# Operand addresses modulo 256 bytes in a two-block transformer kernel's split fp32 matmuls

## The reference, cut to what matters

```
proj = h @ w_in[l]                        # first block: conv, pool and gate branches
mix = merged @ w_out[l]
up = causal_dwconv(h @ w_up[l], w_dw_f[l], b_dw_f[l])
f = (jax.nn.gelu(gt) * v) @ w_down[l]
...
proj = x @ w_in                           # gated delta rule, then swiglu
q, k, v = jnp.split(x @ w_qkv, 3, axis=-1)  # attention, then swiglu
g, u = jnp.split(x @ w13, 2, axis=-1)
return (jax.nn.silu(g) * u) @ w2
```

## The kernel before, in words

| tensor | start before | mod 256 | start in the change | mod 256 |
|---|---|---|---|---|
| raw | 2048 | 0 | 2048 | 0 |
| hi | 47104 | 0 | 47104 | 0 |
| lo | 67584 | 0 | 68224 | 128 |
| ones | 88256 | 192 | 89536 | 192 |
| hh | 89888 | 32 | 91264 | 128 |
| hl | 98080 | 32 | 99456 | 128 |
| fh | 106304 | 64 | 107648 | 128 |
| fl | 110400 | 64 | 111744 | 128 |
| idle | 114496 | 64 | part of ones | 192 |
| crow, xa, h, B, st, ev, Z, sm, cst | 115520 and on | 64 | 116064 and on | 96 |

## Time and profile before

### The profile page before, as it was taken

How to read it: one execution, slowest core, us unless ns; L and a number is a source line. 1 busy time by engine, 2 the same in 40 slices (tenths; PEclk the granted TensorE clock), 3 DMA queues, 4 the chain that set the end, 5 groups by cost and what they waited for, 6 DMA issues and landing times.

```text
span 1039.5 us, 18332 instructions
## 1 busy us (share of the span) xinstructions
PE 1023.4 (98%) x7499; PEld 958.9 (92%) x7499; DVE 754.0 (73%) x1293; ACT 572.9 (55%) x960; POOL 27.5 (3%) x34
## 2 busy tenths in 40 slices
PE   8999999999999999999999999999999999999997
PEld 7999998999999998999987999999899878999996
DVE  6988998899777788877867555555889576555555
ACT  5573447665555586724646445444746565444443
POOL 0000000000100042000000000000000000000000
PEclk9999999999999999999999999999999999999999
DMA  9999873588765533622245555665364426655511
GB/s 370 418 419 370 316 243 124 196 270 274 233 190 193 165 108 115 224 63 80 84 142 186 167 186 191 188 194 186 121 229 158 132 95 250 209 187 183 186 58 41
DMA packets 59603, 201.22 MB, mean 194 GB/s; under 512 B 10496, under 2 KB 10880, under 8 KB 59264
## 3 DMA queue, kind: packets, MB, share of 16 engines
q1 hardware_dynamic: 58368, 199.98, 56.2%
q10 hardware_dynamic: 1152, 0.07, 0.1%
HBM read 198.71 MB, written 1.31 MB: 192 GB/s over the span
## 4 chain that ended last, share of the span: by engine, by line
PE 86%; DVE 10%; ACT 2%; issue 1%; DMA 1%; SPq 0%; DVEq 0%; ACTq 0%
PE ps L632 73%; PE ps L1012 4%; DVE lo L1899 2%; DVE raw L1883 1%; DVE B L2356 1%; PE ps L818 1%; PE ps L720 1%; DVE B L1968 1%; PE ps L771 1%; PE ps L869 1%; DMA B<-in_t 1%; ACT hi L1300 1%; PE ps L806 0%; PE ps L791 0%; DVE sm L2180 0%
## 5 line engine op out<-in xcount | busy, mean ns | idle before, releaser
L1899 DVE TENSOR_TENSOR lo<-raw,hi 128x1024 fp32r<-128x1024 f32 x297 | 360.8, 1222 | 123.3 <-ACT hi L1300 122.6
L632 PE MATMUL ps<-hh,hi 128*128 128x256 f32 x1528 | 432.1, 283 | 2.2 <-DVE hl L1945 1.1
L632 PE MATMUL ps<-hl,hi 128*128 128x256 f32 x1528 | 426.7, 279 | 0.0
L632 PE MATMUL ps<-hh,lo 128*128 128x256 f32 x1528 | 426.7, 279 | 0.0
L1300 ACT ACTIVATE hi<-raw 128x1024 fp32r<-128x1024 f32 x305 | 318.4, 1052 | 50.2 <-PE ps L632 49.1
L632 PEld LDWEIGHTS ps<-hh,hi 128*128 128x128 f32 x1528 | 287.3, 188 | 6.3 <-issue 2.0
L632 PEld LDWEIGHTS ps<-hl,hi 128*128 128x128 f32 x1528 | 287.3, 188 | 1.9 <-issue 0.3
L632 PEld LDWEIGHTS ps<-hh,lo 128*128 128x128 f32 x1528 | 287.3, 188 | 0.0
L632 PE MATMUL ps<-hi,fh 128*128 128x512 f32 x192 | 76.3, 397 | 0.0
L632 PE MATMUL ps<-lo,fh 128*128 128x512 f32 x192 | 75.9, 395 | 0.0
L632 PE MATMUL ps<-hi,fl 128*128 128x512 f32 x192 | 75.8, 395 | 0.0
(11 more groups left out here) (333 smaller groups left out, 1277.4 us busy)
## 6 DMA issues: line engine op xcount, KB each, us to landing
raw<-in_w SPq DMA_DIRECT2D x356, 512.0 KB, 4.3
Z<-in_w SPq DMA_DIRECT2D x9, 512.0 KB, 9.9
B<-in_t SPq DMA_DIRECT2D x2, 512.0 KB, 4.9
B<-in_w SPq DMA_DIRECT2D x2, 512.0 KB, 8.5
h<-in_w SPq DMA_DIRECT2D x2, 512.0 KB, 7.7
xa<-in_x SPq DMA_DIRECT2D x1, 1024.0 KB, 8.6
B<-in_r SPq DMA_DIRECT2D x1, 1024.0 KB, 6.4
out<-h SPq DMA_DIRECT2D x4, 256.0 KB, 2.0
```

Of the source, the lines that this page charges most:

```text
L632: m = g.matmul(o, l, r, start=first and n == 0, stop=last and n == 2, skip_group_check=True)
L1899: g.tensor_tensor(lo[:, j % SPLIT, :], raw[:, PLACE[j] % RAW, :], hi[:, j % SPLIT, :].bitcast(F), ALU.subtract).then_inc(*up("lo", j))
```

## The change

The slots of `hi` and `lo` become 1056 numbers long (4224 bytes, 128 more than a multiple of 256), and `start_of` starts the used 1024 numbers 0 or 128 bytes into the slot, so that all slots of both rings have one residue, 0; for units of the kinds in `MOVING` it is 128. `gap0` and `gap1` get other lengths, `idle` becomes a view of `ones`, and one memset goes. At the end of TensorE's program 30 flipped matmuls are added, at five offsets into `hh`, whose results nobody reads. `idle_rows` is defined and not called.

```
+MOVING = {"gz", "vt", "gout", "bout", "w13r0", "w13r1", "w20", "w21"}
...
-        hi = sb("hi", [P, SPLIT, 1024], FR)
-        lo = sb("lo", [P, SPLIT, 1024], FR)
+        hi = sb("hi", [P, SPLIT, 1056], FR)
+        lo = sb("lo", [P, SPLIT, 1056], FR)
...
-        gap0 = sb("gap0", [P, 24])
+        idle = ones.rearrange("p a b -> p (a b)")[:, 0:S].bitcast(FR)
+        gap0 = sb("gap0", [P, 44])
         hh = sb("hh", [P, NC, S], FR)
         hl = sb("hl", [P, NC, S], FR)
-        gap1 = sb("gap1", [P, 8])
         fh = sb("fh", [P, 4, S], FR)
         fl = sb("fl", [P, 4, S], FR)
-        idle = sb("idle", [P, S], FR)
+        gap1 = sb("gap1", [P, 52])
...
+        def start_of(j, n):
+            return 32 * ((n * SPLIT + j % SPLIT + (UNITS[j][0] in MOVING)) % 2)
+
         def slot(j):
-            return hi[:, j % SPLIT, :], lo[:, j % SPLIT, :]
+            return tuple(w[:, j % SPLIT, start_of(j, n):start_of(j, n) + 1024] for n, w in enumerate((hi, lo)))
...
-            g.memset(idle[:, :].bitcast(F), 1.0).then_inc(*up("fill", "idle"))
...
+            def idle_wide(shift, n, by=0):
+                xh, xl = (x[:, :, :].rearrange("p a b -> p (a b)") for x in (hh, hl))
+                for k in range(n):
+                    a = k * S + shift
+                    three(bank[5][:, :], hi[:, 0, by:by + 512], lo[:, 0, by:by + 512], xh[:, a:a + P], xl[:, a:a + P], True, True,
+                          flip=True)
...
             ffn_tokens("w131", "w21", "w13r1", "x5", x5_free)
+            idle_wide(8, 2)
+            idle_wide(16, 2)
+            idle_wide(24, 2)
+            idle_wide(28, 2)
+            idle_wide(4, 2)
```

More of the change, by code:

```diff
@@ L612, in gpsimd @@
                 s.wait_ge(*at("hi", j))
-                g.tensor_tensor(lo[:, j % SPLIT, :], raw[:, PLACE[j] % RAW, :], hi[:, j % SPLIT, :].bitcast(F),
-                                ALU.subtract).then_inc(*up("lo_pool", j))
+                wh, wl = slot(j)
+                g.tensor_tensor(wl, raw[:, PLACE[j] % RAW, :], wh.bitcast(F), ALU.subtract).then_inc(*up("lo_pool", j))
             v = ofin[:, 0, 512:1024]
@@ L623, in tensor, with idle_rows @@
         def tensor(g, s):
+            def idle_rows(shift, n, by=0):
+                xh, xl = (x[:, :, :].rearrange("p a b -> p (a b)") for x in (hh, hl))
+                for k in range(n):
+                    a = k * S + shift
+                    w = k % 4 * P + by
+                    three(bank[4][:, 0:S], hi[:, 0, w:w + P], lo[:, 0, w:w + P], xh[:, a:a + S], xl[:, a:a + S], True, True)
+            def idle_wide(shift, n, by=0):
+                xh, xl = (x[:, :, :].rearrange("p a b -> p (a b)") for x in (hh, hl))
+                for k in range(n):
+                    a = k * S + shift
+                    three(bank[5][:, :], hi[:, 0, by:by + 512], lo[:, 0, by:by + 512], xh[:, a:a + P], xl[:, a:a + P], True, True,
+                          flip=True)
             def spin(n, b=7):
@@ L1299, in high @@
                         s.wait_ge(*at("unit", j - SPLIT))
-                    g.activation(hi[:, j % SPLIT, :], raw[:, PLACE[j] % RAW, :], ACT.Copy).then_inc(*up("hi", j))
+                    g.activation(slot(j)[0], raw[:, PLACE[j] % RAW, :], ACT.Copy).then_inc(*up("hi", j))
             n_table = [0]
@@ L1898, in low @@
                     s.wait_ge(*at("hi", j))
-                    g.tensor_tensor(lo[:, j % SPLIT, :], raw[:, PLACE[j] % RAW, :], hi[:, j % SPLIT, :].bitcast(F),
+                    g.tensor_tensor(slot(j)[1], raw[:, PLACE[j] % RAW, :], slot(j)[0].bitcast(F),
                                     ALU.subtract).then_inc(*up("lo", j))
```

## The result

The changed kernel takes 1048.18 us (1048.12 to 1048.72, 4 runs) against 1039.09 us beside it: 1.0088 times as long, interval 1.007 to 1.0105, 9.1 us slower. That is inside the stated range and on the wrong side: the forecast was 1016.7.

A forecast was written before the change was run, and what follows sets the result against it. PE was taken as the bound, through line 632's matmul pace. Of 26.6 us less PE work 85%, 22.6 us, would show; with 0.3 for the added matmuls, -22.3 us from 1039.0 gives 1016.7 us, range 1002 to 1052.

The forecast's parts named there:

- The bound and the terms: PE, busy 98%, bounds; line 632's matmul pace changes only through distances; counts times pace changes sum to 26.6 us of PE.
- the price of the plain form at 128: Line 632's plain matmuls at distance 128 take 111.7 ns: 22.5 us less with hh, 0.8 us less with fh.
- the straight line through 0, 32 and 64: Plain paces 120, 116.6 and 113.2 ns fall 3.4 ns per 32 bytes, reaching 109.2 ns at about distance 101.
- The floor: Pace without conflict, from fp32 rows: 109.2 ns for a plain matmul, 216 ns for a flipped one.
- The flipped form: Line 632's 1104 flipped matmuls, moved to distance 0, take 230 ns for 233: 3.3 us less.
- the spins' step: Matmuls of idle by itself, at distance 0, take 10.8 ns over the lowest pace; the same step gives flipped ones 227.
- The share on the path: 85% of PE's 26.6 us gain shows in the time: 22.6 us.
- what is late next: After PE, the split: DVE's subtraction waits 122.6 us for ACT, ACT 49.1 us for slots that PE frees.
- The tail: The 30 added matmuls at the end hide beside the last norm, only just; 0.3 us added.
- falling or least near 80: Added matmuls' flipped paces: falling with distance by the straight line, or least near 80 if distance counts both ways.
- The slower rival: Cyclic reader order, its jump below 128: plain matmuls cost up to 126.2 ns, to 1086 us; chance 0.23, half mild.
- its milder case: Distance 128 lies on a slope at 120 ns for plain matmuls: 15.9 us slower, to 1055; half of chance 0.23.

The follow-up runs named there:

- the true 112: Changed kernel without added matmuls, four operand parts in one tensor starting 16 bytes earlier (plain at 112, flipped at 16); 1025.99 against 1039.48 us before, 0.9872.
- f1_history: Kernel before plus eight pairs of distances behind its end, each three times 24 and 24 plain matmuls; fh at 64 took 113.5 or 117.8 ns.

## Why the prediction was wrong

**The bound and the terms** held. Line 632's pace is what the time hangs on, only the distances differ, and counts times paces give 9.3 of 9.1 us. The layout's 128 in place of the title's 112 was read rightly, and it decided: the true 112 gains 13.5 us.

**The step that failed** is the price of the plain form at 128, "I take 111.7". It was 119.2, 7.5 ns more on 5112 matmuls or 38 us of PE: a term put down as 23 us of gain was 14 us of loss. It failed because the straight line through 0, 32 and 64 was made from three numbers that are no points of one curve. The 120 and the 116.6 are patterns of their distances, and the 113.2 of fh at 64 was one of two patterns at 64, the one mostly found behind hh at 32. A kernel with all of hh at 64 has 117.8, with which there is no line. The trace of the kernel before held warnings, had I looked at more than means: 113.2 is a steady 113, 113, 114, but 116.6 is 120, 113, 116, 118, a cycle of four, and one stretch with fh took 117.8.

**The floor** of 109.2 was not reached by the plain form's mean at any distance; 113.3 is the best seen. The floor of the flipped form, 216, was not reached either: 226.6. That the pace of fp32 rows is open to float32r ones was an inference, and no run bears it out.

**The flipped form** at 0 was taken at 230 and came to 228.8: 4.6 us for 3.3. Right in size. It came from one start in the earlier trace rows; the same trace has 38 such starts, and 27 of them are 229 ns, so the one was typical. The 227 of the spins' step, named as a bound, is what the form settles to behind the kernel's end (226.7).

**The share on the path**, 85%, had no gain to be tried on here. The true 112 gives 13.5 / 17.5 = 77%. The chain of that kernel has only 81% PE:

```profile
PE 81%; DVE 13%; ACT 4%; issue 1%; DMA 0%; SPq 0%; DVEq 0%; ACTq 0%
PE ps L648 69%; PE ps L1028 4%; DVE lo L1915 3%; DVE raw L1899 2%; DVE B L2372 1%; PE ps L834 1%; PE ps L736 1%; ACT hi L1316 1%; DVE B L1984 1%; PE ps L787 1%; PE ps L885 1%; DVE xa L1926 1%; PE ps L822 0%; ACT h L1357 0%; DMA B<-in_t 0%
```

DVE's part of the chain goes from 10 to 13%: the split was what is late next, as the prediction named it. ACT's wait for slots did not tell much: 49.1 us before, 48.9 after, 46.2 at the true 112.

**The tail** was priced at 0.3 and is 0.4. The added matmuls were also to show the curve of the flipped form, falling or least near 80. They showed neither: in the order of their offsets the sixes took 233, 231, 231, 231 and 232 ns, and six starts are too few to settle.

**The slower rival** named the right side, and its milder case put 128 at the spins' 120, near the 119.2 found; it expected 15.9 us of loss where 9.1 were measured, since 0.8 ns less on 5112 matmuls are 4 us, and the flipped form gave 1.3 more. (Its full case adds up to 1087, not 1086.) Its reason, a cyclic order with a jump, is not what the curve shows.

## What to carry to other kernels

When a stream of equal instructions is the bound, look at single starts and not only at their mean: where they repeat in a pattern, as here, a mean at one setting need not say anything of the next, and every setting has to be run. Measure such a table in one run with matmuls behind the kernel's end, give each setting enough of them to settle (twelve were too few here), let each follow several others, prefer one that is reached from all of them, and then run the whole kernel: 192 looked as good as 112 behind the end and was not. And read tensor starts from the built program: padding that is no multiple of the allocator's rounding ends somewhere else, here 16 bytes and 22 us away from the intended place.

## What was not expected of the hardware

- The pace of back-to-back float32r matmuls depends on where moving and loaded operand start modulo 256 bytes: 113.3 to 120.1 ns for 256 columns, 226.6 to 234.8 for 512. The Trainium skill (SBUF — State Buffer, two separate sides) lets TensorE wait for nobody and in its tables gives the weight load a read port of its own. By that no distance should matter; here it does, by up to 6%, though the runs don't show that it is those two reads that wait.
- The same instructions at the same addresses run at 113.3 or 117.8 ns (`f1_history`, fh at 64) and keep the pace for all 24. What ran before them picks one, though not by its distance alone.
- 16 bytes decide (112 against 128: 22 us), and so do 8 (112 against 120: 34 us).
- The fp32 matmuls of 260 columns (L818) showed nothing of it: 219.5 ns before and 219.6 after, at eight distances 32 bytes apart.
- Which part of the chip sets the pattern was not tried; the runs leave it open.
